# A seven-product block scheme for six of 22 slabs of the down projection in a two-layer decoder trunk

## What is computed

```python
def conv_ffn(h, w_up, conv_w, conv_b, w_down):
    S = h.shape[1]
    u = h @ w_up
    up = jnp.pad(u, ((0, 0), (CONV_WIDTH - 1, 0), (0, 0)))
    u = conv_b + conv_w[0] * up[:, 0:S] + conv_w[1] * up[:, 1:S + 1] + conv_w[2] * up[:, 2:S + 2]
    g, val = u[..., :D_FF], u[..., D_FF:]
    return (jax.nn.silu(g) * val).astype(h.dtype) @ w_down
# in each layer:
    y = conv_ffn(h, w_up[layer], conv_w[layer], conv_b[layer], w_down[layer])
    x = x + rmsnorm(y, g_ffn_post[layer])
```

## Time and profile before

| | |
|---|---|
| median of 3 runs | 2471.76 us (2471.75 to 2472.54) |
| profiled execution, its own time | 2470.3 us |
| its span, first to last instruction | 2468.5 us |
| PE busy | 2454.0 us, 99% |
| DVE busy | 1561.9 us, 63% |
| ACT busy | 1271.0 us, 51% |
| down phase of layer 0, of layer 1 | from 990.3 us, from 2221.4 us, 239.5 us each |

### The profile page before, as it was taken

How to read it: one execution, slowest core, us unless ns; L and a number is a source line. 1 busy time by engine, 2 the same in 40 slices (tenths; PEclk the granted TensorE clock), 3 DMA queues, 4 the chain that set the end, 5 groups by cost and what they waited for, 6 DMA issues and landing times.

```text
span 2468.5 us, 34768 instructions
## 1 busy us (share of the span) xinstructions
PE 2454.0 (99%) x12348; PEld 2084.3 (84%) x12348; DVE 1561.9 (63%) x2166; ACT 1271.0 (51%) x1825; POOL 50.7 (2%) x119
## 2 busy tenths in 40 slices
PE   9999999999999999999999999999999999999998
PEld 8888888888888888888888888888888888888887
DVE  6556656677777677544564467566776776775444
ACT  6445555665555555444454455555655555554443
POOL 0000000000000000000000002000000000000000
PEclk9999999999999999999999999999999999999999
DMA  8557455556656665666566665555566666566565
GB/s 294 186 190 256 137 171 170 176 174 186 197 178 194 187 195 181 214 198 193 187 198 187 188 208 166 167 180 173 171 193 191 183 186 195 185 196 202 193 194 167
DMA packets 247007, 468.13 MB, mean 190 GB/s; under 512 B 17520, under 2 KB 20736, under 8 KB 246912
## 3 DMA queue, kind: packets, MB, share of 16 engines
q1 hardware_dynamic: 234640, 447.83, 58.1%
q10 hardware_dynamic: 12272, 19.04, 2.4%
HBM read 464.69 MB, written 2.11 MB: 189 GB/s over the span
## 4 chain that ended last, share of the span: by engine, by line
PE 96%; DVE 2%; ACT 1%; DMA 1%; issue 0%; POOL 0%; DVEq 0%; POOLq 0%; ACTq 0%
PE acc L1557 18%; PE acc L1559 18%; PE acc L1558 18%; PE acc L1578 12%; PE aux L1578 6%; PE acc L1586 6%; PE tp L1578 6%; PE aux L1586 3%; PE tp L1586 3%; DVE w_lo L955 1%; PE tp L1768 1%; PE tp L1602 1%; PE acc L1789 1%; PE aux L1776 0%; DMA g_post<-in_g_mem_post 0%
## 5 line engine op out<-in xcount | busy, mean ns | idle before, releaser
L955 DVE TENSOR_TENSOR w_lo<-raw,w_hi 128x1024 fp32r<-128x1024 f32 x847 | 1022.3, 1222 | 677.5 <-ACT w_hi L442 676.4
L442 ACT ACTIVATE w_hi<-raw 128x1024 fp32r<-128x1024 f32 x847 | 868.7, 1054 | 443.8 <-PE acc L1559 383.1
L1557 PE MATMUL acc<-w_hi,a_hl 128*128 128x512 f32 x1212 | 479.0, 395 | 3.0 <-DVE a_hl L992 3.0
L1559 PE MATMUL acc<-w_hi,a_hl 128*128 128x512 f32 x1212 | 472.7, 390 | 0.0
L1558 PE MATMUL acc<-w_lo,a_hl 128*128 128x512 f32 x1212 | 471.9, 389 | 0.0
L1578 PE MATMUL acc<-a_hl,w_hi 128*128 128x512 f32 x1344 | 417.0, 391 | 0.0
L1578 PEld LDWEIGHTS acc<-a_hl,w_hi 128*128 128x128 f32 x1344 | 241.7, 189 | 40.5
L1557 PE MATMUL acc<-w_hi,hid_hi 128*128 128x512 f32 x704 | 274.1, 389 | 0.0
L1558 PE MATMUL acc<-w_lo,hid_hi 128*128 128x512 f32 x704 | 273.9, 389 | 0.0
L1559 PE MATMUL acc<-w_hi,hid_lo 128*128 128x512 f32 x704 | 273.9, 389 | 0.0
L1586 PE MATMUL acc<-a_hl,w_lo 128*128 128x256 f32 x1344 | 269.9, 282 | 0.0
(11 more groups left out here) (198 smaller groups left out, 2097.4 us busy)
## 6 DMA issues: line engine op xcount, KB each, us to landing
raw<-in_w_up SPq DMA_DIRECT2D x352, 512.0 KB, 3.9
raw<-in_w_down SPq DMA_DIRECT2D x176, 512.0 KB, 4.7
raw<-in_w_in_c SPq DMA_DIRECT2D x96, 512.0 KB, 4.4
raw<-in_w_in_ab SPq DMA_DIRECT2D x95, 512.0 KB, 4.6
raw<-in_w_out_ab SPq DMA_DIRECT2D x32, 512.0 KB, 4.3
raw<-in_w_out_c SPq DMA_DIRECT2D x32, 512.0 KB, 4.6
raw<-in_w_mk SPq DMA_DIRECT2D x16, 512.0 KB, 3.6
raw<-in_w_mq SPq DMA_DIRECT2D x16, 512.0 KB, 3.8
```

What stands on the lines that cost most here:

```text
L442: act.activation(w_hi[:, s], raw[:, s], ACT.Copy).then_inc(hi_ready, 1)
L955: dve.tensor_tensor(w_lo[:, s], raw[:, s], w_hi[:, s].bitcast(F32), ALU.subtract).then_inc(lo_ready, 1)
L1557: pe.matmul(o, hi[:, kt, rows], w_hi[:, slot, j, :], start=(kt == 0), stop=False)
L1559: return pe.matmul(o, lo[:, kt, rows], w_hi[:, slot, j, :], start=False, stop=(kt == kts - 1))
```

## The change

The 22 K slabs of down are taken for two column groups c and c+1 at once, in pairs: p = 0 for groups 0 and 1, p = 1 for groups 2 and 3. In a pair the order is slabs 6 and 7 for c, 6 and 7 for c+1, then 16 sets of one K slab for both groups, then slabs 18 to 21 for c and for c+1. Of the 16 sets the numbers 0, 2, 5, 8, 10 and 13 are "sevens" (K slabs 0 to 5) and the others plain (K slabs 8 to 17). Plain slabs are computed as before.

In a seven the eight block products (two token halves, two K tiles, two column groups) are replaced by seven products of sums of blocks (Winograd's form of Strassen's scheme), each again three matmuls of 512 columns: 21 matmuls for the set and not 24. Its operands:

- seven stationary blocks of hidden sums, made once for each K slab at the end of up and kept in float32 (`hid_f`, `hid_f2`, in the place of `hid_hi` and `hid_lo`); for each seven ACT and DVE split them into `st_hi` and `st_lo` (512 and 384 columns);
- four differences of weight blocks, which DVE makes for each seven from the two `raw` slots (4 x 512 columns, one of them in place in `raw`); ACT and DVE split three of them into `t_hi` and `t_lo` (1536 columns); the fourth goes through the ordinary split.

The staging tiles exist once, so ACT waits with `st_hi` until PE has done the seven before (`seven_used`). The products accumulate in seven banks (`tp`, `aux`, three of `acc`); after the last seven of a pair one copy and four adds put the three shared ones into `yg` (`p1_copy`, `u_sums`), and each of a layer's eight y tiles gets one add of its `acc` bank (`y_add`) ahead of its square. The first three up pairs after the first are unrolled. Some semaphores are shared, which moves no instruction.

```diff
+SEVEN_I = 3
+SEVENS = 2 * SEVEN_I
+PAIR_SLABS = 2 * FF_GS
+HEAD_Q = (SEVENS, SEVENS + 1)
+TAIL_Q = range(FF_GS - TAIL, FF_GS)
+def down_order():
+    plain = list(range(HEAD_Q[-1] + 1, TAIL_Q[0]))
+    sets = len(plain) + SEVENS
+    at = [k * sets // SEVENS for k in range(SEVENS)]
...
 # ScalarE
-                for g in range(D_GROUPS):
-                    for s in range(FF_GS):
...
+                def seven_hi(k, q, c, m):
+                    if c % 2 == 0:
+                        if m == 0:
+                            act.wait_ge(slab_used, n)
+                            act.wait_ge(*LV(L, "hid_lo", SEVEN_I))
+                        else:
+                            act.wait_ge(*LV(L, "seven_used", m))
+                        for to, a in zip(seven_stage(st_hi), seven_sources(q)):
+                            act.activation(to, a, ACT.Copy).then_inc(LS(L, "st_hi"), 1)
+                        split(n + k, (n + k) % RING)
+                    else:
+                        act.wait_ge(*LV(L, "t_sum", 4 * m + 2))
+                        split(n + k, (n + k) % RING)
+                        act.wait_ge(*LV(L, "t_sum", 4 * m + 4))
+                        act.activation(t_hi[:], t_sum[:], ACT.Copy).then_inc(LS(L, "t_hi"), 1)
...
+                for k in range(len(DOWN) - TAIL):
+                    val_tail(FF_GROUPS - 1, k)
...
+                    q, c, m = DOWN[k + AHEAD]
+                    if m is None:
+                        ahead(n + k)
+                    else:
+                        seven_hi(k + AHEAD, q, c, m)
 # VectorE
+            def y_add(sub, g, h, n_done):
+                if n_done is None:
+                    dve.wait_ge(*SV(sub, "y_half", TAIL))
+                else:
+                    dve.wait_ge(slab_used, n_done)
+                dve.wait_ge(*LV(sub[1], "u_out", 4 * (g // 2 + 1)))
+                dve.tensor_tensor(y_cols(h, g), acc[:, g % 2, h, :], y_cols(h, g), ALU.add).then_inc(S(sub, "y_acc"), 1)
...
+                def seven_lo(k, q, c, m):
+                    if c % 2 == 0:
+                        for part, (to, a, hi) in enumerate(zip(seven_stage(st_lo), seven_sources(q), seven_stage(st_hi))):
+                            dve.wait_ge(*LV(L, "st_hi", 2 * m + part + 1))
+                            dve.tensor_tensor(to, a, hi.bitcast(F32), ALU.subtract).then_inc(LS(L, "st_lo"), 1)
...
+                        dve.tensor_tensor(t_sum[:, 2, :], raw[:, s1, 1, :], raw[:, s1, 0, :], ALU.subtract).then_inc(done, 1)
+                        dve.tensor_tensor(raw[:, s1, 0, :], raw[:, s1, 0, :], raw[:, s0, 0, :], ALU.subtract)\
+                            .then_inc(done, 1)
+                        dve.wait_ge(*LV(L, "t_sum", 4 * m + 2))
+                        dve.tensor_tensor(t_sum[:, 0, :], raw[:, s1, 1, :], raw[:, s1, 0, :], ALU.subtract).then_inc(done, 1)
+                        dve.wait_ge(*LV(L, "t_sum", 4 * m + 3))
+                        dve.tensor_tensor(t_sum[:, 1, :], raw[:, s0, 1, :], t_sum[:, 0, :], ALU.subtract).then_inc(done, 1)
+                        split(n + k, s0)
+                    else:
+                        split(n + k, (n + k) % RING)
+                        dve.wait_ge(*LV(L, "t_hi", m + 1))
+                        dve.tensor_tensor(t_lo[:], t_sum[:], t_hi[:].bitcast(F32), ALU.subtract).then_inc(LS(L, "t_lo"), 1)
 # TensorE
+                def seven(k, c, m):
...
+                    pe.wait_ge(lo_ready, n + k + 1)
+                    if c % 2 == 0:
+                        pe.wait_ge(*LV(L, "st_lo", 2 * m + 2))
...
+                        by_weights(tp[:, 0, :], 0, 0, first, last)
+                        by_weights(acc[:, 0, 0, :], 1, 1, False, False).then_inc(slab_used, 1)
+                    else:
+                        by_weights(tp[:, 1, :], 3, 0, first, last)
+                        by_weights(acc[:, 1, 0, :], 6, 1, False, False).then_inc(slab_used, 1)
+                        pe.wait_ge(*LV(L, "t_lo", m + 1))
+                        by_sums(aux[:, 0, :], 4, 0, first, last)
+                        by_sums(acc[:, 0, 1, :], 2, 1, False, False)
+                        by_sums(aux[:, 1, :], 5, 2, first, last).then_inc(LS(L, "seven_used"), 1)
```

More of the change, by code:

```diff
@@ L82 @@
 PHASE, LAYER_SLABS = layer_slabs()
+SEVEN_I = 3
[7 more added lines that the diff above has]
+    at = [k * sets // SEVENS for k in range(SEVENS)]
+    order = []
+    for p in range(D_GROUPS // 2):
+        g = (2 * p, 2 * p + 1)
+        order += [(q, c, None) for c in g for q in HEAD_Q]
+        rest, sevens = iter(plain), iter(range(SEVENS))
+        for k in range(sets):
+            seven = k in at
+            q = next(sevens) if seven else next(rest)
+            order += [(q, c, p * SEVENS + q if seven else None) for c in g]
+        order += [(q, c, None) for c in g for q in TAIL_Q]
+    return order
+DOWN = down_order()
+LAST_SEVEN = max(k for k in range(PAIR_SLABS) if DOWN[k][2] is not None) + 1
 TOTAL_SLABS = LAYERS * LAYER_SLABS
@@ L176, in build @@
         junk_ffn = place("junk_ffn", [P, N], at=a_at)
+        hid_f = place("hid_f", [P, FF_KT, SEQ], at=big_at)
+        hid_f2 = place("hid_f2", [P, FF_KT, SEQ], at=big_at + FF_KT * KB)
+        t_sum = place("t_sum", [P, 3, N], at=a_at + 2 * KB)
+        t_hi = place("t_hi", [P, 3, N], F32R, at=a_at + 8 * KB)
+        t_lo = place("t_lo", [P, 3, N], F32R, at=a_at + 14 * KB)
+        st_hi = place("st_hi", [P, 7, P], F32R, at=a_at + 20 * KB)
+        st_lo = place("st_lo", [P, 7, P], F32R, at=a_at + 24 * KB)
         ident = place("ident", [P, P])
@@ L567, in tail @@
                         y_square(sub, 1, h, e - 2 * MEM_GS)
+                if sub[0] == "ffn":
+                    for h in range(HALF):
+                        y_square(sub, 2, h, None)
                 ahead(e - 3)
@@ L1072, in tail @@
                 ahead(e - 3)
+                if sub[0] == "ffn":
+                    for h in range(HALF):
+                        y_gain(sub, 2, h)
+                    y_add(sub, 3, 0, None)
                 if sub[0] == "mem":
@@ L1457, in _ @@
+                for h in range(HALF):
+                    y_add(ffn, 2, h, n + len(DOWN) - TAIL)
                 if L + 1 < LAYERS:
@@ L1463, in _ @@
             for h in range(HALF):
+                y_gain(SUBS[-1], 2, h)
+            for h in range(HALF):
+                y_add(SUBS[-1], 3, h, e if h else None)
                 y_gain(SUBS[-1], 3, h)
@@ L1941, in _, with products @@
                 up_pair(0, n, True)
-                up_pair(1, n + 2 * GS, False)
-                with pe.Fori(2, FF_GROUPS) as i:
+                for i in range(1, SEVEN_I + 1):
+                    up_pair(i, n + i * 2 * GS, False)
+                with pe.Fori(SEVEN_I + 1, FF_GROUPS) as i:
                     up_pair(i, i * (2 * GS) + n, False)
                 n = n0 + PHASE["down"]
-                for g in range(D_GROUPS):
-                    if g < 2:
-                        u_free(2 * FF_GROUPS + g)
-                    y_free(ffn, g)
-                    for s in range(FF_GS):
-                        if g == 0:
-                            pe.wait_ge(*LV(L, "hid_lo", (SLAB_KT * s) // 4 + 1))
-                        k = g * FF_GS + s
-                        if k >= D_GROUPS * FF_GS - TAIL:
-                            break
-                        slab(n + k, k % RING, g % 2, SLAB_KT * s, FF_KT, hid_hi, hid_lo)
+                def products(o, a_h, a_l, b_h, b_l, first, last=False):
+                    pe.matmul(o, a_h, b_h, start=first, stop=False)
+                    pe.matmul(o, a_h, b_l, start=False, stop=False)
+                    return pe.matmul(o, a_l, b_h, start=False, stop=last)
@@ new lines, in plain @@
+                def plain(k, q, c):
+                    pe.wait_ge(lo_ready, n + k + 1)
+                    slot, first = (n + k) % RING, q == HEAD_Q[0]
+                    for h in range(HALF):
+                        rows = slice(h * P, (h + 1) * P)
+                        for j in range(SLAB_KT):
+                            kt = SLAB_KT * q + j
+                            last = products(acc[:, c % 2, h, :], hid_hi[:, kt, rows], hid_lo[:, kt, rows], w_hi[:, slot, j, :],
+                                            w_lo[:, slot, j, :], first and j == 0, kt == FF_KT - 1)
+                    last.then_inc(slab_used, 1)
@@ new lines, in _ @@
+                for k in range(len(DOWN) - TAIL):
+                    q, c, m = DOWN[k]
+                    p, r = k // PAIR_SLABS, k % PAIR_SLABS
+                    if r in (0, 2):
+                        if p == 0:
+                            u_free(2 * FF_GROUPS + c)
+                        else:
+                            pe.wait_ge(*SV(ffn, "y_acc", r + 2))
+                    if p == 0:
+                        pe.wait_ge(*LV(L, "hid_lo", (SLAB_KT * q) // 4 + 1))
+                    if m is None:
+                        plain(k, q, c)
+                    else:
```

(1 more changed line is left out.)

157 lines of the change are left out of this document (121 added, 36 removed).

## The result

The changed kernel takes 2479.03 us (median of 7 runs, 2477.47 to 2480.94); the kernel before takes 2470.92 beside it (7 runs). The ratio is 1.0033, 95% interval 1.0023 to 1.0042: slower by 8.1 us, where 3.1 were forecast (from a kernel of 2471.76). A second set of runs gave 2479.63 and 1.0031.

What follows compares the result with a forecast made beforehand. PE, busy 99% of the span, was taken to bound the kernel. The terms -16.3 + 2 x 8.8 + 0.75 + 1.1 = +3.1 us gave 2474.9 us, range 2466 to 2484 (the forecast's own 2470 to 2479).

Steps and rivals of the forecast that it cites:

- Matmuls removed: On PE in down: 24 sevens of 21 matmuls for 24 save 16.3 us, 8.16 a layer.
- The seven's chain on DVE: In each seven in down: six small DVE operations, at gaps of 0.60 or 0.72, take 3.71 us.
- Start of down: First sevens of each down: PE waits for DVE, busy with the last up group and slabs; 6.6 us a layer.
- Sevens with one plain pair ahead: Steady part of down: single staging makes PE lose 0.6 us plus 0.1 at `t_lo`, three more times a layer.
- The adds of groups 0 to 2: In down: DVE's y adds for these groups are hidden by its idle time per slab, at no cost.
- Change of layer: Between layers: group 3's add stands before each token half's tail; 1.1 us, bounds 0 and 1.5.
- The 0.3 to spare: At the change of layer: the first transpose has some 0.3 us spare, so 0.4 of the 0.75 shows.
- End: After the last matmul: group 3's add of 0.69 and a signal stand before square and gain; 0.75 us.
- Rival 2: Start of down: PE's clock falls after the long wait, 2 to 3 us a layer, giving 2480; chance 0.16.
- Rival 1: In down: DVE's new work is hidden, giving 2457.4, or 2468 in a partial form; chance 0.12 together.
- Rival 3: In down: loads for sevens come 1 us later, near 5 us a layer, giving 2484; chance 0.12.

Runs made afterwards that it cites:

- second trace: The changed kernel run once more with nothing altered, against the kernel before: 2479.63 us, ratio 1.0031.

## Why the prediction was right, and where its sizes were off

- **Matmuls removed, -16.3.** Right: 36 fewer in each down, 0.2267 apart.
- **The seven's chain on DVE, 3.71.** Right: 3.72. The gaps are 0.60 without a wait for the one before and 0.72 with it, where the rule of the Trainium skill weighed in the forecast ("VectorE: DVE Perf Modes", section "The DRAIN you can't avoid") would make them alike. The forecast left out that the same section has a next operation start earlier when it is not held; the 0.60 agrees with that, and the 0.12 more behind a semaphore goes against its statement that the semaphore costs nothing extra.
- **Start of down, 6.6 a layer.** Measured 6.3, step for step. The late sevens took it away.
- **Sevens with one plain pair ahead, 0.7 each.** Measured 0.6, at the three places named. Those with two plain pairs ahead, put at nothing, lost nothing in the first trace and 0.85 us once in the second, by the late load.
- **The adds of groups 0 to 2 "hidden alike".** This step failed, for group 2: the forecast put it at nothing, and it cost 0.67 us in each down. The add itself was hidden; ACT's squares, which now wait for it, stand ahead of a split. The forecast asked what hides the added operation, and not what is queued behind the one that waits for it. Moving them gave it back.
- **Change of layer, 1.1, bounds 0 to 1.5.** Mis-sized: 2.7 us in the first trace, and the trace without the last add gives 2.5. Two parts were missing. GpSimd is held for 0.5 us in each half (1.1 of PE's waits, by the run with the add in PSUM), and the second add queues behind `a_hl` on DVE (0.91 after the last matmul for 0.43). The 0.3 to spare was about right, since the first half showed 0.98 for an add of 0.75 and a hold of 0.5.
- **End, 0.75.** Mis-sized: 1.22. The add itself was right: the end is 8.49 us with the add in PSUM and 7.76 without the add, 0.73 apart. What was missing is GpSimd again, 0.70. (Together 1.43. The last store takes 0.2 us less than in the kernel before, 2.5 for 2.7 from issue to landing, which leaves the 1.22.)
- **Rival 2, the clock.** Its mechanism exists and its price was wrong. Of twelve downs with these first waits (six traces of five kernels), five went on at 1.2 GHz after the long one, for seven or eight matmuls and not fifteen, and at no cost, as DVE's backlog decided the next start. It cost 1.6 us at a place that was not named, the change of layer, in three of the six traces that have the three waits of the changed kernel there (0.8, 1.05 and 1.05), and in none of the three with the shorter ones (0.48 in place of the first 1.05). With so few traces this points to the waits and does not prove it. The Trainium skill, "TensorE: Matmul & The Clock Gate", section "HAM oscillation — how this bites in real kernels", says that matmul bursts parted by waits restart at half clock each time; its example has longer waits than these, and the traces agree for some executions of one kernel and not for others.
- **Rival 1.** No: DVE's work showed where it was forecast.
- **Rival 3.** Not in the first trace: loads came after DVE asked for them (16.0 us in twelve waits), but not on PE's path. In the second it is there with 0.85 us, at one seven, where its price was 5 a layer.

The sum, with what was measured: 3.1 as forecast; less 0.1 for the waits inside down that were foreseen; 1.3 for the last slabs; 1.6 for the change of layer; 0.5 for the end: 6.4, which is what the first trace shows; and 1.6 for the clock in some executions. The second trace has 8.9 with the clock (1.55) and the late load (0.85). The medians, 8.1 and 8.8, lie between the two traces. How many executions have the one or the other is not counted, so the medians are not taken apart further.

That the measured time lies near rival 2's 2480 is chance: the clock gave 1.6 of the 5 us that this rival asked for, at another place, and the rest of the distance is the last slabs, the change of layer and the end.

## What to carry to other kernels

When an operation is put in between two others, ask three things: what hides it, what is queued behind whoever now waits for it, and what its operands do to a neighbour. A new step at the end of a phase counts once for each half, and for its place in its engine's queue as well as for its length. And where new work comes in bursts, put the bursts where the engine has room: moving the sevens of the first pair by two or three sets was worth 10 us, where all sevens together save 16.3.

## What the runs showed of the hardware

- GpSimd's 128x1 operation took 0.70 us beside a DVE operation with two SBUF operands and 0.19 beside one with a PSUM operand. The Trainium skill, "GPSIMD Engine Reference", section "1. Specifications", lists the SBUF interfaces as shared with VectorE, with contention when VectorE has two SBUF inputs; the traces agree, at 0.5 us each time.
- TensorE's granted clock fell to 0.50, the 1.2 GHz level, after a wait of PE of 2.7 us with one of 0.9 before it (five of twelve downs), and after 0.8, 1.05 and 1.05 us close together (three of six traces), in some executions of a program and not in others. In the second set of runs of the changed kernel, three with a mean granted clock of 0.999 had a mean span of 2476.3 us and three with 0.997 had 2478.6.
- Up to the first down, two executions of the kernel before differ by 2.1 us; behind it they are the same to 0.03. In the changed kernel one load of 512 KB took 5.2 us in one execution and 7.4 in the next, and PE waited for it in the second alone.
